# Norm weights moved from the mixers into the merge, x times D and two levels of scores moved to ScalarE, B transposed into another bank

## The chip, the cores and the metric

One core of a Trainium2 chip runs the whole program. The metric is device time in microseconds (us), median of several runs. The engines are called as in the profile: PE (TensorE, matrix products), DVE (VectorE), ACT (ScalarE), POOL (GpSimd), SP (the engine that here only issues transfers). "Bank" is one of PE's eight result banks in PSUM, 128 partitions by 512 float32.

## The reference

One layer of a hybrid decoder over 1024 tokens, width 1024: a token mixer with three branches (GLA, HGRN2, Mamba-2 SSD), merged by gates, and then a mixture of 32 experts. What this change touches, cut down:

```
# GLA and HGRN2, chunk by chunk (4 + 4 heads): o = intra-chunk scores @ v + decayed q @ state
y_gla  = rms_norm(o_gla,  gla_norm_w)  * silu(gr)
y_hgrn = rms_norm(o_hgrn, hgrn_norm_w) * silu(hg)
# SSD: 16 heads in 4 groups
y = ssd_chunked_scan(xs, dt, a_neg, bm, cm)
y = (y + ssm_d[:, None] * xs) * silu(sz)
y_ssm = rms_norm(y in 4 groups, ssm_norm_w)
g = sigmoid(gates)
merged = g0*(y_gla @ w_br_gla) + g1*(y_hgrn @ w_br_hgrn) + g2*(y_ssm @ w_br_ssm)
out = merged @ w_out
```

## The kernel before

The program runs in stages, each a block with its own streams of instructions per engine, ordered by hand; engines meet only by semaphores. The stages are: norm and decays, projection, `mixers`, `merge_and_route`, two expert stages, and `finish`. A float32 matrix product of the large stages is three products of rounded parts (hi*hi, hi*lo, lo*hi).

`mixers` walks over 8 chunks of 128 tokens (`body(c)` on each engine). Beside the mixers' own work PE computes the gate projection there: `fill(n)` issues the next n of its matmuls (128x512, line 1602). 24 of them make a half (`LATE_MM`), 8 a slot (`SLOT`), and a chunk has 15 slots between its own steps. All halves inside the chunks use bank 7, so the first matmul of a half waits until ACT has copied the half before out (`late(h)`, line 1258). After a copy ACT also rounds the next gate weights (`late_hi`, line 1251) or, for even h, issues the load of later ones (`late_load`, line 1246); that issue waits for DVE's `late_lo` (line 1375), and all that stands behind it in ACT's stream waits too. Odd chunks (1, 3, 5, 7) have the `late_load` at their first copy, even chunks the `late_hi`.

The steps of a chunk, in PE's order: the diagonal scores (1641); `intra(c-1, 1)`, second half of the SSD product of the chunk before (1669); levels 0 to 6 of the GLA/HGRN2 scores (`level`, 1627), a recursive halving in which level lv has blocks of h = 64 >> lv tokens; after level 2 the SSD product C*B (`cb`, 1690, into `ssm_ps`, bank 6); after level 3 the SSD state update (`ssm_state`, 1649); then `ssm_means(c-1)` (1657), a product with a matrix of equal entries that gives the mean squares for the last chunk's SSD norm; the transposes of B (1701) into the same bank 6; level 4; the transposes of x (1710) into `mid_ps` (banks 2 and 3); levels 5 and 6; transposes of k (1720); the outputs `o` (1730, 1731); `inter` (1735); the state update (1741); `intra(c, 0)`; the mean squares of the GLA/HGRN2 norm (1749).

For a level, DVE multiplies k and q by decays (`factors(lv)`, 1468 to 1470) and, when PE has its scores, copies those under the level's mask into `score` with a predicated copy (`scores_in(lv)`, 1486). DVE also does `gla_hgrn_out` (1439, 1443: times the reciprocal root, then eight instructions for weight and gate), `x_in_sum` (1405: eight instructions, x times D plus y), `z_gated` (1411), the subtraction `wd` (1517), the masked C*B (`cbm`, 1523) and `ssm_out` (1454: eight instructions, weight and reciprocal root). `wd` is the first to read `wmat` (in the profile `dn_raw_a`), which SP loads with a broadcast of `b_ssm` over 128 partitions (`load_bb`, 1 MB); SP issues it when PE has done `intra(c-1, 1)`. ACT computes the exponentials of each level (`relative`, 1270, 1271), the SSD squares (`ssm_squares`, 1283, wanted by `ssm_means`), the differences of `wmat` (1310), the copy of B's transposes (`bT`, 1330), the reciprocal roots (1275, 1277; 1287, 1289) and the squares of `o` (1337).

`merge_and_route` starts by splitting y into rounded parts: ACT `upper_y` (2118), DVE `rest_y` (2217), 16 pieces of 128x1024.

Of the kernel before, what the change touches and what calls it, by code (L numbers as in the profile page):

```python
# [957 lines left out]
def mixers(nc, io, dr, h_hi, h_lo, l_raw, l_hi, l_lo, w_place, xz_place, stored, early):  # L958
# [6 lines left out]
    NS = NL + 2  # L965
    CT = 6
    QT = 8
    NH = GLA_HEADS + HG_HEADS
    N_PAR = 5
# [4 lines left out]
    with ExitStack() as ctx:  # L974
# [35 lines left out]
        nw, nw_s, d_col = sb("nw", [P, NH]), sb("nw_s", [P, 8]), sb("d_col", [P, 8])  # L1010
# [39 lines left out]
        score_ready = sem("score_ready")  # L1050
        eb6_ready = sem("eb6_ready")
# [28 lines left out]
        intra_used = sem("intra_used")  # L1080
        xd_ready = sem("xd_ready")
# [21 lines left out]
        def _(sp):  # L1103
# [61 lines left out]
            sp.dma_start(nw[:, 0:4], io["gla_norm_w"].rearrange("(k p) -> p k", p=P)).then_inc(par_in, 16)  # L1165
            sp.dma_start(nw[:, 4:8], io["hgrn_norm_w"].rearrange("(k p) -> p k", p=P)).then_inc(par_in, 16)
            sp.dma_start(nw_s[:], io["ssm_norm_w"].rearrange("(k p) -> p k", p=P)).then_inc(par_in, 16)
            for a in range(2):
                sp.dma_start(d_col[a * HALF:(a + 1) * HALF, :], io["ssm_d"][a::2].unsqueeze(0).to_broadcast([HALF, 8]))\
                    .then_inc(par_in, 16)  # L1170
            for c in range(NCH):
# [68 lines left out]
        def _(act):  # L1240
# [50 lines left out]
            def body(c):  # L1291
# [4 lines left out]
                relative(c, 3)  # L1296
                relative(c, 4)
                late(h0)
# [16 lines left out]
                late(h0 + 1)  # L1315
                if c:
                    ssm_scale(c - 1)
# [9 lines left out]
                act.wait_ge(bT_ps_ready, c + 1)  # L1327
                if c:
                    act.wait_ge(hupd_ready, c)
                nc.scalar.copy(flat(bT[:]), ssm_ps).then_inc(bT_ready, 1)  # L1330
# [37 lines left out]
        def _(dve):  # L1368
# [68 lines left out]
            def gla_hgrn_out(c):  # L1437
# [13 lines left out]
            def ssm_out(c):  # L1451
                dve.wait_ge(rs2_ready, c + 1)
                for k in range(8):
                    ins = stt(yb[:, k, :], yt[:, k, :], nw_s[:, k:k + 1], rs2[:, k // 2, :], ALU.mult, ALU.mult)
                ins.then_inc(yb_ready, 1)

            def body(c):
                b, h0 = c % 2, PREFIX + PER_CHUNK * c

                def factors(lv):  # L1460
                    h, e = LEVELS[lv], ex[(NE * c + lv) % 3]
                    dve.wait_ge(e_ready, NE * c + lv + 1)
                    v = lambda x: x.rearrange("p (n w) -> p n w", w=2 * h)
# [8 lines left out]
                def diagonal_in(a):  # L1472
                    n = NS * c + a
                    dve.wait_ge(sc_ready, n + 1)
# [5 lines left out]
                def scores_in(lv):  # L1480
                    n, h = NS * c + 2 + lv, LEVELS[lv]
                    dve.wait_ge(sc_ready, n + 1)
                    dve.wait_ge(score_ready, n)
                    dve.sem_inc(passed, 1)
# [18 lines left out]
                scores_in(0)  # L1503
# [3 lines left out]
                scores_in(1)  # L1507
# [62 lines left out]
            for c in range(NCH):  # L1570
                if c == 1:
                    dve.wait_ge(par_in, 16 * N_PAR)
# [10 lines left out]
        def _(pe):  # L1583
# [31 lines left out]
            def level(c, lv):  # L1615
# [3 lines left out]
                pe.wait_ge(score_ready, NS * c + lv + 1)  # L1619
# [40 lines left out]
            def intra(c, s):  # L1660
                if s == 0:
                    pe.wait_ge(w_ready, c + 1)
                    pe.wait_ge(bT_ready, c + 1)
# [9 lines left out]
            def body(c):  # L1673
# [51 lines left out]
                pe.wait_ge(score_ready, NS * c + NS)  # L1725
# [60 lines left out]
def merge_and_route(nc, io, dr, ident, w_raw, y_raw, up_raw, up_at, xe, recs, recs_in, gather, early, kept_sem):  # L1786
# [32 lines left out]
    with ExitStack() as ctx:  # L1819
# [265 lines left out]
        def _(act):  # L2085
# [24 lines left out]
            def upper_y(p):  # L2110
# [7 lines left out]
                nc.scalar.copy(y_hi[:, q * PK:(q + 1) * PK, :], y_part(p)).then_inc(y_hi_ready, 1)  # L2118
# [36 lines left out]
            upper_w0(first, w0_loaded, w0_hi_ready)  # L2155
            for p in range(4):
                upper_y(p)
# [41 lines left out]
        def _(dve):  # L2199
# [13 lines left out]
            def rest_y(p):  # L2213
                dve.wait_ge(y_hi_ready, p + 1)
                q = p % PIECES
                ks = slice(q * PK, (q + 1) * PK)
                tt(y_lo[:, ks, :], y_part(p), y_hi[:, ks, :].bitcast(F32), ALU.subtract).then_inc(y_ready, 1)  # L2217
# [101 lines left out]
            rest_w0(first, w0_hi_ready, w0_ready)  # L2319
            for p in range(4):  # L2320
# [743 lines left out]
def build(nc, io, out):  # L3064
# [16 lines left out]
    with ExitStack() as ctx:  # L3081
# [11 lines left out]
        early = {name: kept_sem(f"early_{name}") for name in ("w0", "w0_rest", "y0", "y1")}  # L3093
# [75 lines left out]
```

## Time and profile before

| | us |
|---|---|
| median of 3 runs | 2035.61 |
| lowest and highest run | 2033.6, 2041.8 |
| span of the profiled execution | 2040.4 |
| mixer stage, chunks 0 to 7 (first diagonal to last `intra`) | 608.2 to 1066.2 |
| PE busy, whole span | 1925.7 (94%) |
| DVE busy | 1472.5 (72%) |
| ACT busy | 1048.0 (51%) |

The span runs from the first to the last recorded instruction. The profiled execution's own time is not listed apart from it; its span lies between the lowest and the highest run, 4.8 above the median. Busy time of an engine is the sum of its instructions; "idle before" in the rows below is the time in which an engine had nothing running just before an instruction, and the name behind the arrow is what ended that time. The granted clock is 1.00 when PE runs at 2.4 GHz and 0.50 at 1.2 GHz.

### The profile page before, as it was taken

The numbers are of one execution on the slowest core, as the hardware profiler recorded it, in microseconds if no ns is written. First come the engines' busy times: TensorE is split into PE (matmuls) and PEld (weight loads), VectorE is DVE, ScalarE is ACT, GpSimd is POOL, SyncE is SP. The second block draws the span as 40 slices with busy tenths as digits, with TensorE's granted clock in tenths as the row PEclk, the third lists the DMA queues.
The fourth block names the chain that finished last, engine by engine and source line by source line (L and its number), as shares of the span: only waits on it lengthen the run. The fifth ranks groups of instructions, "written<-read, shape, count | busy, mean of one in ns | idle before, by whom it ended". The sixth has DMA issues, their size and how long they took to land. (4 is left out here: it accounts for less than half of the span.)

```text
span 2040.4 us, 26797 instructions
## 1 busy us (share of the span) xinstructions
PE 1925.7 (94%) x10602; PEld 1576.7 (77%) x10603; DVE 1472.5 (72%) x1687; ACT 1048.0 (51%) x1234; POOL 218.3 (11%) x173
## 2 busy tenths in 40 slices
PE   6999999999999999999998999995999999999993
PEld 5789888888977777777776888874788888888881
DVE  5876467667227888788775656556889988999875
ACT  5234344444224545444444334223777887888763
POOL 3310000000030000000001000012122222222210
PEclk9999999999999999999998999997999999999996
DMA  5242332432355557656537654543999999999986
GB/s 168 86 145 73 114 104 97 131 104 93 107 145 158 151 160 168 167 127 152 160 115 282 206 204 182 229 178 138 349 376 384 389 386 385 389 386 387 387 331 259
DMA packets 212415, 436.11 MB, mean 214 GB/s; under 512 B 28018, under 2 KB 151042, under 8 KB 184770
## 3 DMA queue, kind: packets, MB, share of 16 engines
q1 hardware_dynamic: 179394, 355.68, 50.3%
q10 hardware_dynamic: 20864, 53.49, 7.5%
q0 software_dynamic: 12032, 25.22, 3.2%
q8 instruction: 85, 1.39, 0.3%
q14 instruction: 40, 0.33, 0.0%
HBM read 369.67 MB, written 81.43 MB: 221 GB/s over the span
## 5 line engine op out<-in xcount | busy, mean ns | idle before, releaser
L1602 PE MATMUL psum<-h_hi,l_hi 128*128 128x512 f32 x384 | 158.5, 413 | 4.9 <-PEq L58 3.3
L1602 PE MATMUL psum<-h_lo,l_hi 128*128 128x512 f32 x384 | 159.8, 416 | 0.0
L1602 PE MATMUL psum<-h_hi,l_lo 128*128 128x512 f32 x384 | 157.9, 411 | 0.0
L2741 DVE TENSOR_TENSOR gu_lo<-up_raw,gu_hi 128x2048 fp32r<-128x2048 f32 x64 | 146.3, 2288 | 13.2 <-ACT gu_hi L2684 13.2
L2684 ACT CAST gu_hi<-up_raw 128x2048 fp32r<-128x2048 f32 x64 | 122.1, 1909 | 35.0 <-PE u_ps L2813 35.0
L1258 ACT COPY l_out<-psum 128x512 f32<-128x512 f32 x48 | 28.1, 585 | 170.3 <-PE psum L1602 162.3
L2457 PE MATMUL mpsum<-y_hi,wb_hi 128*128 128x512 f32 x256 | 103.3, 403 | 10.1 <-DVE y_lo L2217 9.1
L2813 PE MATMUL g_ps<-gu_hi,xeT_hi 128*128 128x512 f32 x256 | 105.0, 410 | 5.8 <-DVE xeT_lo L2750 5.8
L806 DVE TENSOR_TENSOR w_lo<-w_raw,w_hi 128x512 fp32r<-128x512 f32 x90 | 61.9, 689 | 65.5 <-ACT w_hi L662 65.5
L662 ACT CAST w_hi<-w_raw 128x512 fp32r<-128x512 f32 x90 | 55.7, 622 | 91.9 <-PE ps L931 91.4
L2457 PE MATMUL mpsum<-y_lo,wb_hi 128*128 128x512 f32 x256 | 101.7, 397 | 0.0
L2457 PE MATMUL mpsum<-y_hi,wb_lo 128*128 128x512 f32 x256 | 101.6, 397 | 0.0
L2813 PE MATMUL g_ps<-gu_hi,xeT_lo 128*128 128x512 f32 x256 | 101.6, 397 | 0.0
L2813 PE MATMUL g_ps<-gu_lo,xeT_hi 128*128 128x512 f32 x256 | 101.4, 396 | 0.0
L2813 PE MATMUL u_ps<-gu_hi,xeT_lo 128*128 128x512 f32 x256 | 99.7, 389 | 0.0
L2813 PE MATMUL u_ps<-gu_hi,xeT_hi 128*128 128x512 f32 x256 | 99.6, 389 | 0.0
L2813 PE MATMUL u_ps<-gu_lo,xeT_hi 128*128 128x512 f32 x256 | 99.6, 389 | 0.0
L3123 POOL DMA_INDIRECT xe<-s_h,recs x32 | 88.6, 2770 | 32.4 <-PE xT_ps L2784 14.9
L1602 PEld LDWEIGHTS psum<-h_hi,l_hi 128*128 128x128 f32 x384 | 73.2, 191 | 21.9 <-issue 7.0
L2741 DVE TENSOR_TENSOR gu_lo<-gate_raw_a,gu_hi 128x2048 fp32r<-128x2048 f32 x32 | 73.4, 2293 | 22.2 <-ACT gu_hi L2684 22.2
L1602 PEld LDWEIGHTS psum<-h_hi,l_lo 128*128 128x128 f32 x384 | 73.5, 191 | 18.8 <-issue 3.3
L2662 POOL DMA_INDIRECT s_pairs<-ye,recs x32 | 41.4, 1293 | 431.3 <-ACT ye L2701 417.9
(465 smaller groups left out, 5419.0 us busy)
## 6 DMA issues: line engine op xcount, KB each, us to landing
up_raw<-moe SPq DMA_DIRECT2D x62, 1024.0 KB, 8.1
gate_raw_a<-moe SPq DMA_DIRECT2D x33, 1024.0 KB, 8.4
gate_raw<-moe SPq DMA_DIRECT2D x33, 1024.0 KB, 8.4
dn_raw_a<-moe SPq DMA_DIRECT2D x31, 1024.0 KB, 7.2
dn_raw<-moe SPq DMA_DIRECT2D x31, 1024.0 KB, 8.0
w_raw<-w_in SPq DMA_DIRECT2D x26, 1024.0 KB, 6.1
l_raw<-w_gates ACTq DMA_DIRECT2D x24, 512.0 KB, 5.4
s_gates<-l_out ACTq DMA_DIRECT2D x48, 256.0 KB, 4.0
```

The costliest lines, as they stand in the source:

```text
L662: nc.scalar.copy(slot_hi[g], source(n, g)).then_inc(hi_ready, 1)
L806: ins = tt(slot_lo[g], source(n, g), slot_hi[g].bitcast(F32), ALU.subtract).then_inc(split_ready, 1)
L1258: nc.scalar.copy(l_out[h % 2][:], psum[:, late_bank(h), :]).then_inc(l_evicted, 1)
L1602: ins = nc.tensor.matmul(psum[:, bank, :], w[t % 2][:, k, :], x[:, k, half * 512:half * 512 + 512], start=i == 0, stop=i == LATE_MM - 1, s ...
L2457: ins = nc.tensor.matmul(ps[:, br, :], w[:, k * P:(k + 1) * P], y[:, k, :], start=k == k0 and q == 0, stop=k == k1 - 1 and q == 2)
L2662: pool.indirect_dma_start(out=dr["pairs"], out_offset=bass.IndirectOffsetOnAxis(ap=recs[:, e, 1:2], axis=0), in_=ye[b][:], in_offset=None, ...
L2684: nc.scalar.copy(gu_hi[p][:], gu_raw[p][:]).then_inc(gu_hi_ready, 1)
L2741: nc.vector.tensor_tensor(gu_lo[p][:], gu_raw[p][:], gu_hi[p][:].bitcast(F32), ALU.subtract).then_inc(gu_ready, 1)
L2813: ins = nc.tensor.matmul(ps[:], x[:, (p - at) * GK + k, :], w[:, k, :], start=p == at and k == 0 and q == 0, stop=p == at + GU // 2 - 1 an ...
L3123: nc.gpsimd.indirect_dma_start(out=xe[e % 2][:], out_offset=None, in_=dr["h2"], in_offset=bass.IndirectOffsetOnAxis(ap=recs[:, e, 0:1], ax ...
```

## The change

- The three norm weights leave the mixers. `gla_hgrn_out` multiplies by the gate in one instruction instead of eight, and `ssm_out` likewise by the reciprocal root. The weights are loaded into `y_weight` and applied in the merge: `upper_y` becomes two scaled activations for a piece, `rest_y` two instructions of multiply and subtract.
- x times D: ACT scales `x_in` in place (`x_scaled`, eight activations, behind `late(h0+3)` and ahead of the squares of `o`), and DVE's `x_in_sum` becomes one addition.
- B's transposes go to the second half of `mid_ps` (bank 3) instead of bank 6. They wait for `ms_read` and no longer for `cbm_ready`. ACT's copy `bT` moves from behind the exponential of `wmat` to right behind `late(h0+1)`, ahead of `ssm_scale`. x's transposes now wait for `bT_ready`.
- `ssm_means` moves behind level 4.
- The scores of levels 0 and 1 are copied by ACT as plain blocks (`outer_scores`: one copy of 64 partitions x 512, two of 32 partitions x 256), behind `relative(3)` and `relative(4)`; DVE's `scores_in(0)` and `scores_in(1)` go. PE's levels 2 and 3 wait for ACT's copies (`outer_ready`) in place of DVE's, and DVE's `factors(2)` and `factors(3)` get a wait of their own for the level that last read their buffers.

```diff
-    N_PAR = 5
+    ON_ACT = 2
+    NM = NS - ON_ACT
+    N_PAR = 2
...
+            def outer_scores(c, lv):
+                h = LEVELS[lv]
+                act.wait_ge(sc_ready, NS * c + 2 + lv + 1)
+                act.wait_ge(score_ready, NM * c + 2)
+                if c:
+                    act.wait_ge(o_ready, c)
+                for n in range(CH // (2 * h)):
+                    j, i = slice(2 * h * n, 2 * h * n + h), slice(2 * h * n + h, 2 * h * (n + 1))
+                    ins = nc.scalar.copy(score[j, :].rearrange("p (a t) -> p a t", t=CH)[:, :, i],
+                                         sc_ps[lv % 2][j, :].rearrange("p (a t) -> p a t", t=HALF)[:, :, n * h:(n + 1) * h])
+                ins.then_inc(outer_ready, 1)
...
+            def x_scaled(c):
+                if c == 0:
+                    act.wait_ge(par_in, 16 * N_PAR)
+                act.wait_ge(xT_ready, c + 1)
+                for k in range(8):
+                    ins = nc.scalar.activation(x_in[:, k, :], x_in[:, k, :], ACT.Copy, scale=d_col[:, k:k + 1])
+                ins.then_inc(xs_ready, 1)
...
                 relative(c, 3)
+                outer_scores(c, 0)
                 relative(c, 4)
+                outer_scores(c, 1)
                 late(h0)
...
                 late(h0 + 1)
+                act.wait_ge(bT_ps_ready, c + 1)
+                if c:
+                    act.wait_ge(hupd_ready, c)
+                nc.scalar.copy(flat(bT[:]), mid_ps[:, 512:1024]).then_inc(bT_ready, 1)
                 if c:
                     ssm_scale(c - 1)
...
                 late(h0 + 3)
+                x_scaled(c)
...
             def x_in_sum(c):
                 dve.wait_ge(intra_used, 2 * c + 2)
-                for k in range(8):
-                    ins = stt(yt[:, k, :], x_in[:, k, :], d_col[:, k:k + 1], yt[:, k, :], ALU.mult, ALU.add)
-                ins.then_inc(xd_ready, 1)
+                dve.wait_ge(xs_ready, c + 1)
+                tt(yt[:], x_in, yt[:], ALU.add).then_inc(xd_ready, 1)
...
-                for h in range(NH):
-                    ins = stt(ya[:, h, :], g_in[:, h, :], nw[:, h:h + 1], ya[:, h, :], ALU.mult, ALU.mult)
-                ins.then_inc(ya_ready, 1)
+                tt(ya, g_in[:], ya, ALU.mult).then_inc(ya_ready, 1)
...
                     dve.wait_ge(e_ready, NE * c + lv + 1)
+                    if 2 <= lv < 2 + ON_ACT:
+                        dve.wait_ge(sc_ready, NS * c + lv + 1)
...
-                scores_in(0)
                 factors(2)
                 if c:
                     intra_in(c - 1, 1)
-                scores_in(1)
                 dec(i0 + 5)
...
                 if c:
-                    ssm_means(c - 1)
-                pe.wait_ge(cbm_ready, c + 1)
+                    pe.wait_ge(ms_read, c)
                 for g in range(SSM_GROUPS):
-                    ins = nc.tensor.transpose(ssm_ps[:, g * P:(g + 1) * P], bc_in[:, g, :], ident[:])
+                    ins = nc.tensor.transpose(mid_ps[:, 512 + g * P:512 + (g + 1) * P], bc_in[:, g, :], ident[:])
                 ins.then_inc(bT_ps_ready, 1)
                 fill(SLOT)
                 level(c, 4)
+                if c:
+                    ssm_means(c - 1)
                 fill(SLOT)
                 pe.wait_ge(x_loaded, 16 * (c + 1))
+                pe.wait_ge(bT_ready, c + 1)
...
-                nc.scalar.copy(y_hi[:, q * PK:(q + 1) * PK, :], y_part(p)).then_inc(y_hi_ready, 1)
+                for a in range(PK):
+                    k = q * PK + a
+                    ins = nc.scalar.activation(y_hi[:, k, :], y_part(p)[:, a, :], ACT.Copy, scale=y_weight[:, k:k + 1])
+                ins.then_inc(y_hi_ready, 1)
...
-                tt(y_lo[:, ks, :], y_part(p), y_hi[:, ks, :].bitcast(F32), ALU.subtract).then_inc(y_ready, 1)
+                for a in range(PK):
+                    k = q * PK + a
+                    ins = stt(y_lo[:, k, :], y_part(p)[:, a, :], y_weight[:, k:k + 1], y_hi[:, k, :].bitcast(F32), ALU.mult, ALU.subtract)
+                ins.then_inc(y_ready, 1)
```

How PE's stream stands around the moved steps in chunk 1, before: between the state update (1649) and level 4 (the next 1627) come two slots of filling (1602), and between the slots the means (1657, of the chunk before) and B's transposes (1701); the waits are those of the first instruction of a step.

```order
L1649 MATMUL psum<-xdt,bT 128x256 x3
L1602 MATMUL psum<-h_hi,l_lo 128x512
...
L1657 MATMUL psum<-y_out,mean_b 128x512 [waits ms_read,sq2_ready]
L1657 MATMUL psum<-y_out,mean_b 128x512
L1701 MATMUL psum<-ident_m,bc_in 128x128 [waits cbm_ready]
L1701 MATMUL psum<-ident_m,bc_in 128x128 x3
L1602 MATMUL psum<-h_lo,l_hi 128x512
```

And the same place in the changed kernel, where 1676 is the state update, 1624 the filling, 1726 B's transposes, 1654 a level and 1684 the means.

```order
L1676 MATMUL psum<-xdt,bT 128x256 x3
L1624 MATMUL psum<-h_hi,l_lo 128x512
...
L1726 MATMUL psum<-ident_m,bc_in 128x128 [waits ms_read]
L1726 MATMUL psum<-ident_m,bc_in 128x128 x3
L1624 MATMUL psum<-h_lo,l_hi 128x512
...
L1654 MATMUL psum<-q_lv,k_lv 64x2x32 [waits score_ready,qk_ready]
```

The means now stand behind level 4, and B's transposes wait for something that ACT did at the chunk's start.

ACT's stream of chunk 1 in the changed kernel, from the exponentials of level 3 to the squares of the SSD output:

```order
L1273 ACTIVATE ex<-ex 128x48x8 [waits d_ready]
L1274 ACTIVATE ex<-ex 128x48x8
L1284 COPY score<-psum 64x8x64 [waits o_ready,score_ready,sc_ready]
L1273 ACTIVATE ex<-ex 128x96x4 [waits d_ready]
L1274 ACTIVATE ex<-ex 128x96x4
L1284 COPY score<-psum 32x8x32 [waits o_ready,score_ready,sc_ready]
L1284 COPY score<-psum 32x8x32
L1261 COPY l_out<-psum 128x512 [waits l_stored0,l_done]
L1263 DMA s_gates<-l_out 128x512 [waits l_evicted]
L1249 DMA l_raw<-w_gates 128x1024 [waits l_split]
L1273 ACTIVATE ex<-ex 128x192x2 [waits d_ready]
L1306 ACTIVATE y_out<-yt 128x1024 [waits yt_ready]
```

The three copies (1284) are new there; the order of the rest is as before.

## Rows read from the trace of the kernel before

**Rows 1.** stretches, chunks 1 to 7: length, busy by engine, clock, DMA, GB/s

```profile
660.34:718.69 58.35, 55.94 (x447) 43.02 (x446) 48.15 (x82) 27.96 (x52) 0.00 (x0) 0.97 0.54 151
718.69:776.72 58.03, 55.52 (x448) 43.61 (x447) 47.21 (x81) 27.15 (x51) 0.00 (x0) 0.97 0.56 163
776.72:834.98 58.26, 55.85 (x448) 43.11 (x447) 48.14 (x82) 27.97 (x52) 0.00 (x0) 0.97 0.63 151
834.98:893.33 58.35, 55.55 (x447) 43.60 (x446) 47.24 (x81) 27.16 (x51) 0.00 (x0) 0.97 0.61 160
893.33:951.30 57.97, 54.47 (x449) 42.45 (x448) 48.22 (x82) 27.96 (x52) 0.00 (x0) 1.00 0.62 153
951.30:1009.50 58.20, 55.55 (x449) 43.56 (x448) 47.17 (x81) 27.17 (x51) 0.00 (x0) 0.97 0.65 162
1009.50:1066.00 56.50, 54.09 (x447) 42.51 (x446) 43.37 (x73) 26.33 (x48) 0.00 (x0) 1.00 0.34 105
```

**Rows 2.** waits of PE in the mixer stage: us, times, longest

```profile
PE psum L1657 <- ACT y_out L1283: 9.6, 4, 2.4
PE psum L1701 <- DVE cbm L1523: 9.1, 4, 2.8
```

**Rows 3.** timeline of PE, chunks 3 and 4: start, duration, idle before

```profile
797.61 3.58 PE L1657 MATMUL psum<-y_out,mean_b 128*128 128x512 f32 x4 [2.41 <-ACT y_out L1283]
...
849.59 1.99 PE L1649 MATMUL psum<-xdt,bT 128*128 128x256 f32 x8
853.28 1.88 PE L1657 MATMUL psum<-y_out,mean_b 128*128 128x512 f32 x4
857.96 0.66 PE L1701 MATMUL psum<-ident_m,bc_in 128*128 128x128 f32 x4 [2.80 <-DVE cbm L1523]
...
889.66 1.88 PE L1749 MATMUL psum<-y_out,mean_a 128*128 128x512 f32 x4
```

**Rows 4.** busy time by stretch, behind a wait of chunk 2

```profile
743.00:746.40 3.40, 3.40 (x29) 2.50 (x29) 3.40 (x7) 0.72 (x2) 0.00 (x0) 0.52 1.11 311
```

**Rows 5.** timeline of DVE, chunk 4

```profile
842.36 0.73 DVE L1486 COPY_PREDICATED score<-mask,psum 128x512 f32<-128x512 uint8 x1
...
848.45 2.20 DVE L1405 SCALAR_TENSOR_TENSOR yt<-gate_raw_a,d_col,yt 128x128 f32<-128x128 f32 x8
850.69 1.22 DVE L1411 TENSOR_TENSOR yt<-yt,gate_raw_a 128x1024 f32<-128x1024 f32 x1
853.33 0.18 DVE L1517 TENSOR_TENSOR wd<-dn_raw_a,b_dt 128x16 f32<-128x16 f32 x1 [1.41 <-DMA dn_raw_a<-s_b_ssm]
...
855.62 0.55 DVE L1470 TENSOR_TENSOR q_lv<-q_in,ex 128x384 f32<-128x384 f32 x1
```

**Rows 6.** timeline of ACT, chunk 3

```profile
786.84 0.58 ACT L1258 COPY l_out<-psum 128x512 f32<-128x512 f32 x1 [3.33 <-PE psum L1602]
...
795.61 0.56 ACT L1270 ACTIVATE ex<-ex 128x384 f32<-128x384 f32 x1 [8.19 <-DVE l_lo L1375]
...
796.51 1.04 ACT L1283 ACTIVATE y_out<-yt 128x1024 f32<-128x1024 f32 x1
...
798.76 2.45 ACT L1310 ACTIVATE dn_raw_a<-dn_raw_a,b_dt 128x128 f32<-128x128 f32 x8
...
823.07 1.02 ACT L1337 ACTIVATE y_out<-psum 128x1024 f32<-128x1024 f32 x1 [1.47 <-PE psum L1731]
```

**Rows 7.** issues of load_bb, chunks 3, 4, 5, then all: size, us to landing

```profile
dn_raw_a<-s_b_ssm SPq DMA_DIRECT2D x1, 1024.0 KB, 14.9
...
dn_raw_a<-s_b_ssm SPq DMA_DIRECT2D x1, 1024.0 KB, 16.3
...
dn_raw_a<-s_b_ssm SPq DMA_DIRECT2D x1, 1024.0 KB, 18.4
...
dn_raw_a<-s_b_ssm SPq DMA_DIRECT2D x8, 1024.0 KB, 16.0
```

**Rows 8.** timeline of PE, start of the merge

```profile
1095.08 0.76 PE L2457 MATMUL mpsum<-y_hi,wb_hi 128*128 128x512 f32 x1 [9.07 <-DVE y_lo L2217]
```

More of the change, by code:

```diff
@@ L955, in late_bank, with mixers @@
     return 7
-def mixers(nc, io, dr, h_hi, h_lo, l_raw, l_hi, l_lo, w_place, xz_place, stored, early):
+def mixers(nc, io, dr, h_hi, h_lo, l_raw, l_hi, l_lo, w_place, xz_place, y_weight, stored, early):
     LEVELS = [64 >> n for n in range(7)]
@@ L1050, in mixers @@
         score_ready = sem("score_ready")
+        outer_ready = sem("outer_ready")
         eb6_ready = sem("eb6_ready")
@@ L1080, in mixers @@
         intra_used = sem("intra_used")
+        xs_ready = sem("xs_ready")
         xd_ready = sem("xd_ready")
@@ L1170, in _ @@
                     .then_inc(par_in, 16)
+            for (k0, k1), name in (((0, 4), "gla_norm_w"), ((4, 8), "hgrn_norm_w"), ((8, 16), "ssm_norm_w")):
+                sp.dma_start(y_weight[:, k0:k1], io[name].rearrange("(k p) -> p k", p=P)).then_inc(early["yw"], 16)
             for c in range(NCH):
@@ L1452, in ssm_out @@
                 dve.wait_ge(rs2_ready, c + 1)
-                for k in range(8):
-                    ins = stt(yb[:, k, :], yt[:, k, :], nw_s[:, k:k + 1], rs2[:, k // 2, :], ALU.mult, ALU.mult)
-                ins.then_inc(yb_ready, 1)
+                grouped = lambda x: x.rearrange("p (g a) t -> p g a t", a=2)
+                tt(grouped(yb), grouped(yt[:]), rs2[:].unsqueeze(2).to_broadcast([P, SSM_GROUPS, 2, CH]), ALU.mult).then_inc(yb_ready, 1)
             def body(c):
@@ L1472, in diagonal_in @@
                 def diagonal_in(a):
-                    n = NS * c + a
-                    dve.wait_ge(sc_ready, n + 1)
+                    n = NM * c + a
+                    dve.wait_ge(sc_ready, NS * c + a + 1)
                     if n:
@@ L1480, in scores_in @@
                 def scores_in(lv):
-                    n, h = NS * c + 2 + lv, LEVELS[lv]
-                    dve.wait_ge(sc_ready, n + 1)
+                    n, h = NM * c + 2 + lv - ON_ACT, LEVELS[lv]
+                    dve.wait_ge(sc_ready, NS * c + 2 + lv + 1)
                     dve.wait_ge(score_ready, n)
+                    if lv == ON_ACT:
+                        dve.wait_ge(outer_ready, ON_ACT * (c + 1))
                     dve.sem_inc(passed, 1)
@@ L1618, in level @@
                 pe.wait_ge(qk_ready, NE * c + lv + 1)
-                pe.wait_ge(score_ready, NS * c + lv + 1)
+                if lv < ON_ACT:
+                    pe.wait_ge(score_ready, NM * c + lv + 1)
+                elif lv < 2 * ON_ACT:
+                    pe.wait_ge(outer_ready, ON_ACT * c + lv - ON_ACT + 1)
+                else:
+                    pe.wait_ge(score_ready, NM * c + lv - ON_ACT + 1)
                 ql = q_lv[lv % 2][:].rearrange("p (a n) -> p a n", n=HALF)
@@ L1724, in body @@
                 pe.wait_ge(q_dec_ready, c + 1)
-                pe.wait_ge(score_ready, NS * c + NS)
+                pe.wait_ge(score_ready, NM * c + NM)
+                pe.wait_ge(outer_ready, ON_ACT * c + ON_ACT)
                 if c:
@@ L2319, in _ @@
             rest_w0(first, w0_hi_ready, w0_ready)
+            dve.wait_ge(early["yw"], 48)
             for p in range(4):
@@ L3092, in build @@
         dn_first, gate_first = many(1, "dn_raw_a", [P, DK, D]), many(1, "gate_raw_a", [P, GK, FF])
-        early = {name: kept_sem(f"early_{name}") for name in ("w0", "w0_rest", "y0", "y1")}
+        early = {name: kept_sem(f"early_{name}") for name in ("w0", "w0_rest", "y0", "y1", "yw")}
+        y_weight = ctx.enter_context(nc.sbuf_tensor("y_weight", [P, 2 * KT], F32, side="right"))
         with ExitStack() as front:
@@ L3107, in build @@
             l_raw, l_hi, l_lo = ([l[:, b] for b in range(2)] for l in late_parts)
-            mixers(nc, io, dr, h_hi, h_lo, l_raw, l_hi, l_lo, flat(dn_first[0]), flat(gate_first[0]), stored, early)
+            mixers(nc, io, dr, h_hi, h_lo, l_raw, l_hi, l_lo, flat(dn_first[0]), flat(gate_first[0]), y_weight, stored, early)
         ident = ctx.enter_context(nc.sbuf_tensor("ident", [P, P], F32))
```

18 lines of the change are left out of this document (4 added, 14 removed).

## The prediction, made before the changed kernel ran

> **What bounds the kernel now.** I cut the trace into the mixer stage's chunks first. A chunk takes about 58 us and PE is busy in all but 2 to 4 us of it, while DVE and ACT have 10 and 30 us to spare [rows 1]. So PE's stream sets the time, and only its waits and slow stretches can be taken away. The list of waits gives 9.6 us in four waits of the means (1657) for ACT's squares and 9.1 us in four waits of B's transposes (1701) for DVE's masked C*B: 18.7 us in chunks 1 to 7 [rows 2]. The odd chunks wait at the means, the even ones at the transposes, chunk 5 at both (chunks 3 and 4: [rows 3]).
>
> The waits cost more than themselves. After chunk 3's wait the four records of the means take 3.58 us in place of 1.88 [rows 3]; after chunk 2's wait a stretch of 3.4 us ran at 0.52 of full speed, 1.2 GHz [rows 4]. A stretch at half clock gives back half its length, 1.7 us. The mean clock is 0.97 in five of the seven chunks and 1.00 in chunks 5 and 7 [rows 1], so I count five: 8.5 us. All told 18.7 + 8.5 = **27.2 us** can go here. Everything before and behind the stage is left alone, but for the start of the merge.
>
> What are the waited-for engines late with? In chunk 3 ACT stands 8.19 us before level 5's exponentials (1270) because the load it must issue first waits for DVE's l_lo; the squares (1283) come behind it, at 796.51, and PE starts the means at 797.61 [rows 3, 6]. In chunk 4 it is DVE that is late: eight instructions for x times D from 848.45, the product with z at 850.69, and then `wd`, which stands 1.41 us until the transfer of `load_bb` has landed, at 853.33 [rows 5]. Behind `wd` come the factors of level 4 (the last begins at 855.62) and the masked C*B that the transposes want.
>
> **The change part by part.**
>
> *Order on PE.* B's transposes no longer wait for DVE, but for a logarithm that ACT does at the chunk's start. The means move behind a slot, level 4, and need the squares some 3 us later relative to PE. With DVE's l_lo 3.3 us earlier (next paragraph) the squares of chunk 3 end near 794.3, and the means start near 798.4. Both old waits go: -18.7 us, and -8.5 with them.
>
> *DVE.* Each of the three eight-fold groups takes 2.20 us and becomes one instruction like the product with z, 1.22 [rows 5]: about 1.0 less each, 3 in a chunk. Two predicated copies of 0.73 (0.6 start to start) go: 1.2. Of these, 1.0 (`gla_hgrn_out`), 1.2 (scores) and 1.0 (`x_in_sum`) lie ahead of `wd`: DVE reaches it 3.3 us sooner. The rest comes late in the chunk, where DVE waits for PE anyway, and is worth nothing.
>
> *ACT.* The trace has no block copy of scores. The nearest row is the copy of a half, 128x512 in 0.58 us [rows 6]; the two small ones have half of that per partition, so I take 0.58 + 2 x 0.35 = 1.3, between 0.7 (if a start overlaps the one before) and, at most, two predicated copies of DVE for each level, 2.9. They sit where ACT stands idle 3.33 us before the half's copy [rows 6], so the cover is gone only above 3.3 us; then the half's copy, and the first filling of the next half that waits for it, come later by the excess. x times D: the eight activations of 1310 on the same shape take 2.45 us together [rows 6]; bounds 2.4 and 3.1. They stand ahead of the squares of `o`, for which ACT had 1.47 us of idle time in chunk 3, so these come 1.0 us (bounds 1.0 to 1.7) later than 823.07 + 1.02. PE reads them in the product at the chunk's end, which in chunk 4 starts at 889.66, 54.7 after the chunk's start; 824.1 is 47.4 after chunk 3's start [rows 1, 3, 6]. Seven us of cover: nothing. Copying B's transposes earlier is the same copy at another place, 0.58 us; it delays `ssm_scale`, for which PE's transposes of x wait. Counting ACT from `wd` (exponentials 1.3, differences 2.45, copy of the half 0.6, in odd chunks the cast 1.5, then 0.6 and the logarithm 0.7) gives 7.2 us after `wd`, against 7.4 on PE from the factors of level 4 (2.9 after `wd`; level 0.8, means 1.9, slot 1.9): 0 in my sum, up to 0.5 a chunk if a step is longer.
>
> *What is late next.* PE will reach level 4 earlier, and its factors stand behind `wd`, which waits for a transfer that DVE's gain cannot hasten. In chunk 4 PE would get there so: filling ended at 853.28, the transposes take 0.45 beyond, the next slot 1.9 (the slot between the state update's end at 851.4 and 853.28 [rows 3]): 855.65, which is 20.65 after the chunk's start at 834.98 [rows 1]. The factors end at 855.62 + 0.55 = 856.17, 2.84 after `wd`. Their load was issued 2.07 us after the chunk's start (853.33 less its 16.3 us to landing [rows 5, 7]). So level 4 waits 2.07 + d + 2.84 - 20.65 = d - 15.7 us, with d the time to landing: the median of the eight is 16.0, chunks 3 and 7 are at 14.9, and chunk 5 had 18.4 [rows 7]. That makes 0.3 in most chunks and 2.7 in chunk 5: about 4 us. In odd chunks one thing is added. ACT's load of gate weights, 512 KB, has gone out only behind DVE's l_lo, when `load_bb` of chunk 3 had landed (776.72 + 2.07 + 14.9 = 793.7, while the exponential behind the load's issue begins at 795.61 [rows 1, 6, 7]); 3.3 us earlier it falls into it. In the even chunks such a load goes out just ahead of `load_bb`, and d is 16.3 where chunk 3 has 14.9 [rows 7]: I take 1.3 for it in the odd chunks, that is 2 us more over the stage (chunk 3 and 7 have 0.8 of slack). Of 4 and 6 I take 5, and one stretch at half clock behind the longest wait, 1.7.
>
> On that point the Trainium skill has a rule ("DMA: Bandwidth & Descriptors", Queues, rings and completion order): each transfer engine goes round between the queues that have work, packet by packet, while one queue's descriptors are taken in order. By that rule x and z, issued 3.3 us earlier on SP's own queue, would not hold `load_bb` up, and ACT's load would. The trace agrees so far: the even chunks' d is longer by 1.4. If SP's loads shared too, the third rival below would be the sum.
>
> *Merge.* A piece's cast becomes two activations of half the length and DVE's subtraction two instructions; PE's 9.07 us of idle time there [rows 8] end with the first piece. I add 0.2 us, between 0 and 1: only the first piece is waited for, and half instructions cost a start more. The three small loads are the same number as before on the same queue, and the merge reads them 400 us later.
>
> **Sum.** -27.2 + 5 + 1.7 + 0.2 = -20.3 us. The profiled execution's span, 2040.4, would become 2020.1; the median of the runs lies 4.8 below that span, and from it I get 2035.6 - 20.3 = 2015.3, say **2015**.
>
> **The rivals.** 0.5% is 10.2 us, about what a measurement of this kernel can tell from no change.
>
> 1. *Forecast*: both waits go, a short one at level 4 comes. 2015, own range 2010 to 2022. Chance 0.58.
> 2. *Nothing is late next.* `load_bb` lands as in chunks 3 and 7, d = 14.9, since the stage's transfers spread otherwise. Then 27 us go: 2008.5. For it: two of seven chunks. Against it: five chunks are later. 0.14.
> 3. *`load_bb` is stretched part of the way* by x, z and the gate weights, all issued 3.3 us earlier: d grows by half of that in every chunk, 1.65, and the waits at level 4 sum to 4 + 7 x 1.65 - 1.6 = 14, with three stretches at half clock 19. The gain is 8: 2027.5, which is "same". For it: chunks 4 and 5 have the longer d, and in both x's load went out with DVE's product of z, before `load_bb` had landed [rows 5]. Against: chunk 4's d is explained by the load ahead of it. 0.15.
> 4. *Slower: `load_bb` is stretched by the whole 3.3 us.* Level 4 waits 4 + 7 x 3.3 - 1.6 = 25.5 us, each wait now as long as those of before, with seven stretches at half clock, 12: 37.5 come, 27.2 go, 2046. From d near 18 on it breaks even (16 us of waits and seven stretches), and from 19.5 on the kernel is slower by more than 0.5%. 0.06.
> 5. *ACT carries too much*: the score copies cost over 3.3 us, or `ssm_scale` comes 1 to 2 us late for x's transposes, and 1.5 us a chunk with some slow stretches eat 14: 2029, "same". ACT is only half busy [rows 1], but its waits are in order. 0.07.
>
> Faster by over 0.5% (below 2025.4): cases 1 and 2 and a part of 3 and 5, 0.78. Within: 0.16. Slower: 0.06. The range 2007 to 2028 leaves out case 4 and the ends of 2, 3 and 5.
>
> **What the profile will show.** Right: chunks of 54 to 55 us at a clock of 1.00 in most; no idle time before the means and before B's transposes; `wd` waiting 2 to 4 us for the transfer in every chunk; a wait of 0 to 1.5 us at level 4 for DVE's q_lv, in chunk 5 perhaps more; DVE's busy time 30 us less, ACT's 30 us more. Wrong: waits of over 2 us at level 4 (rivals 3, 4, with d of 18 and more), or at x's transposes for ACT's logarithm, or at the first filling behind a half for its copy (rival 5); or chunks that stay at 58 us.

## The result, and the profile after

The changed kernel takes 2025.68 us, the median of 4 runs (2025.02 to 2026.66); the kernel before took 2036.06 (2033.6 to 2041.8) in the same comparison. The ratio is 0.9944, 95% interval 0.993 to 0.9957: 10.4 us gained, about half of the 20.3 forecast. The profiled execution has a span of 2024.9 us.

First the page's busy times. PE carries what it carried before; DVE has lost work and ACT has taken it.

```profile
PE 1919.6 (95%) x10602; PEld 1577.3 (78%) x10603; DVE 1440.2 (71%) x1519; ACT 1080.9 (53%) x1338; POOL 216.5 (11%) x173
```

The stretches of chunks 1 to 7, to be laid beside [rows 1] (length, busy by engine, granted clock, DMA share, GB/s):

```profile
660.61:715.83 55.22, 53.75 (x448) 42.68 (x447) 43.79 (x59) 31.50 (x63) 0.00 (x0) 1.00 0.53 160
715.83:773.27 57.44, 55.37 (x448) 43.69 (x447) 42.88 (x58) 30.73 (x62) 0.00 (x0) 0.97 0.66 164
773.27:827.25 53.98, 53.76 (x447) 42.66 (x446) 43.80 (x59) 31.47 (x63) 0.00 (x0) 1.00 0.71 164
827.25:882.31 55.06, 53.78 (x448) 42.68 (x447) 42.65 (x58) 30.62 (x62) 0.00 (x0) 1.00 0.62 170
882.31:940.04 57.73, 55.42 (x448) 43.45 (x447) 43.98 (x59) 31.53 (x63) 0.00 (x0) 0.97 0.63 154
940.04:997.37 57.33, 55.43 (x447) 43.39 (x446) 42.87 (x58) 30.74 (x62) 0.00 (x0) 0.97 0.72 163
997.37:1052.00 54.63, 53.52 (x447) 42.67 (x446) 38.90 (x50) 29.82 (x59) 0.00 (x0) 1.00 0.41 109
```

They sum to 391.4 us where they summed to 405.7: 14.3 less. DVE is busy for 4.4 us less in a chunk, ACT for 3.5 more. The clock is 0.97 in three chunks (2, 5 and 6) where it was in five.

PE's waits in the mixer stage and up to the merge:

```profile
PE psum L1654 <- DVE q_lv L1494: 10.4, 7, 2.3
PE mpsum L2493 <- DVE y_lo L2251: 9.3, 1, 9.3
```

Both lines of [rows 2] are gone. In their place stands one, seven times: the products of level 4 (line 1654) wait for DVE's factors `q_lv`. The second line is the start of the merge, 0.2 more than in [rows 8]. Chunk 5 shows the new wait at its longest, first on PE, then on DVE (start, duration, idle before):

```profile
905.34 1.04 PE L1654 MATMUL psum<-q_lv,k_lv 128*64 128x64 f32 x24 [2.31 <-DVE q_lv L1494]
906.31 3.47 PE L1684 MATMUL psum<-y_out,mean_b 128*128 128x512 f32 x4
```

```profile
893.99 1.22 DVE L1431 TENSOR_TENSOR yt<-gate_raw_a,yt 128x1024 f32<-128x1024 f32 x1
895.25 1.22 DVE L1436 TENSOR_TENSOR yt<-yt,gate_raw_a 128x1024 f32<-128x1024 f32 x1
902.37 0.18 DVE L1541 TENSOR_TENSOR wd<-dn_raw_a,b_dt 128x16 f32<-128x16 f32 x1 [4.76 <-DMA dn_raw_a<-s_b_ssm]
902.59 0.72 DVE L1512 COPY_PREDICATED score<-mask,psum 128x512 f32<-128x512 uint8 x1
904.73 0.55 DVE L1494 TENSOR_TENSOR q_lv<-q_in,ex 128x384 f32<-128x384 f32 x1
```

DVE now has a single 1.22 us instruction where eight took 2.20 [rows 5]; it is ready at 897.6 and stands still at `wd` until `load_bb` has landed. Behind it PE waits 2.31 us, and the means that follow take 3.47 us: half clock, 1.2 GHz. The longest-waiting lines of DVE and ACT:

```profile
DVE wd L1541 <- DMA dn_raw_a<-s_b_ssm: 31.9, 7, 6.2
ACT wd L1329 <- DVE wd L1541: 20.7, 7, 5.3
```

Last, the load itself: first chunk 3's, then chunk 5's, then the seven of the stage with their median, to be laid beside [rows 7].

```profile
dn_raw_a<-s_b_ssm SPq DMA_DIRECT2D x1, 1024.0 KB, 15.9
...
dn_raw_a<-s_b_ssm SPq DMA_DIRECT2D x1, 1024.0 KB, 18.0
...
dn_raw_a<-s_b_ssm SPq DMA_DIRECT2D x7, 1024.0 KB, 17.1
```

Chunk by chunk, with before's for comparison (the loads from the same view of that chunk's first 6 us, `wd` from DVE's timeline, less the chunk's start):

| chunk | 1 | 2 | 3 | 4 | 5 | 6 | 7 |
|---|---|---|---|---|---|---|---|
| `load_bb` to landing, before | 15.8 | 16.0 | 14.9 | 16.3 | 18.4 | 16.1 | 14.8 |
| to landing, after | 17.1 | 17.7 | 15.9 | 16.9 | 18.0 | 17.5 | 16.8 |
| `wd` begins, after the chunk's start, before | 18.39 | 18.07 | 18.38 | 18.35 | 20.45 | 18.18 | 18.38 |
| `wd` begins, after | 19.20 | 19.81 | 17.94 | 19.03 | 20.06 | 19.63 | 18.85 |
| wait at level 4, after | 1.47 | 2.08 | 0.22 | 1.28 | 2.31 | 1.90 | 1.11 |
| the forecast's d - 15.7 | 1.4 | 2.0 | 0.2 | 1.2 | 2.3 | 1.8 | 1.1 |

The formula held to 0.1 us in all seven. Its input did not: d is 17.1 on average in place of 16.0. The rows of `wd` hold a surprise. DVE is ready for it 2.9 to 3.4 us sooner than before in every chunk, and still it begins 0.6 us later on average (19.2 in place of 18.6): in chunks 1, 3 and 7 of the kernel before it had not waited for the load at all.

### The profile page after: what moved, and what is told of

The parts are those of the page before. It is cut to its first block and busy times, and to the rows that moved or that the text cites. A ratio compares the mean times of both kernels' runs of the same rounds, so it can differ in the third digit from the quotient of the medians.

```text
span 2024.9 us, 26770 instructions
## 1 busy us (share of the span) xinstructions
PE 1919.6 (95%) x10602; PEld 1577.3 (78%) x10603; DVE 1440.2 (71%) x1519; ACT 1080.9 (53%) x1338; POOL 216.5 (11%) x173
## 5 line engine op out<-in xcount | busy, mean ns | idle before, releaser
L1624 PEld LDWEIGHTS psum<-h_lo,l_hi 128*128 128x128 f32 x384 | 73.2, 191 | 18.4 <-issue 4.1
```

The source lines that it names most:

```text
L1624: ins = nc.tensor.matmul(psum[:, bank, :], w[t % 2][:, k, :], x[:, k, half * 512:half * 512 + 512], start=i == 0, stop=i == LATE_MM - 1, s ...
```

## The experiments

Each stands beside runs of the kernel before on its own chip (medians 2038.0, 2038.4 and 2039.8), so the ratios are what to compare. "The stage" below is the mixer stage in each kernel's trace, from the first diagonal to the last `intra`: 459.0 us before, 442.8 in the changed kernel.

**Does `v`, loaded just ahead of `load_bb`, take its time?** The changed kernel with the two loads exchanged:

```diff
-                    sp.wait_ge(upd_ready, c + 1)
-                    load_v(n)
                     sp.wait_ge(intra_ready, 2 * c + 2)
                     load_bb(n)
+                    sp.wait_ge(upd_ready, c + 1)
+                    load_v(n)
```

> The changed kernel, with the load of v issued behind load_bb instead of ahead of it; nothing else is different, and v is wanted only some 35 us later. Theory (load_bb's landing sets level 4): v no longer stands ahead in the queue, so load_bb lands 1.5 to 2 us sooner after its issue (15 to 15.5 us in place of 17.1), the 10.4 us of waits at level 4 shrink to 1 to 3, the three stretches at half clock go with them: 2025.7 - 13 = about 2013. Rival (the rest of the chunk's time is lost elsewhere, in ACT's or DVE's order): no change within 2 us, level 4 waits for something else.

2028.56 us (2024.09 to 2030.1), ratio 0.9946 (0.9922 to 0.997). The loads take 16.1 to 17.7 us, the waits at level 4 sum to 10.9: as in the changed kernel, and not the 13 us less that were expected. The place of `v` does not matter. Whether `v` takes some of the load's time in either place is not shown: ahead of it, `v` still lands up to 3.8 us into the load, and behind it, 0.4 us later, it is in flight beside all of it.

**Do the loads issued behind it?** In the changed kernel SP holds x and z back until `load_bb` has landed, and with them all that stands behind them in its stream, first the store of y (`ya`), which otherwise goes out 1 us behind x:

```diff
                     sp.wait_ge(yt_ready, c + 1)
+                    sp.wait_ge(bb_loaded, 16 * (n + 1))
                     load_x(n)
                     load_z(n)
```

> The changed kernel, with SP waiting until load_bb has landed before it issues the loads of x and z and all that follows in its stream. Theory A (SP's own loads, issued 3.3 us sooner, stretched load_bb from 16.0 to 17.1): the time to landing goes back to 15 to 16 us, the waits at level 4 fall from 10.4 to about 4, one stretch at half clock stays: about 2016. Theory B (one queue is served in order, the gate weights of ACT's queue stretched it): load_bb unchanged at 17 us, 2025 to 2027. Rival to both: x comes too late for its transposes and PE waits there: above 2027.

2018.34 us (2014.55 to 2018.9), ratio 0.9897 (0.9869 to 0.9924). PE's and DVE's waits, and the load:

```profile
PE psum L1655 <- DVE q_lv L1495: 4.6, 6, 1.5
```

```profile
DVE wd L1542 <- DMA dn_raw_a<-s_b_ssm: 25.8, 7, 5.1
```

```profile
dn_raw_a<-s_b_ssm SPq DMA_DIRECT2D x7, 1024.0 KB, 16.2
```

The load lands 0.9 us earlier by the median, PE's wait falls from 10.4 to 4.6, no stretch at half clock is left in chunks 1 to 7, and 7 us come back by the medians, 9 in the stage (433.7 us). By chunk the loads take 16.2, 16.7, 15.9, 16.3, 17.1, 16.1 and 15.4 us: less than in the changed kernel in six of the seven, the same in chunk 3. The kernels of the next experiment agree: the median is 16.2 us where x and z go out as late as before (`order_only`), and 17.4 where they go out as early as in the changed kernel (`work_only`). So what SP issues later on its own queue did stretch the load ahead of it; which of x, z and the store does it is not shown. That disagrees with the use which the prediction made of the Trainium skill ("DMA: Bandwidth & Descriptors", Queues, rings and completion order): from descriptors taken in order on one queue it concluded that later ones would not hold an earlier one up.

**Which part of the change brings the gain?** `order_only` is the kernel before with the three moves on PE and ACT alone (B's transposes into the other bank without the wait for the masked C*B, their copy early, the means behind level 4); `work_only` is the changed kernel with those three undone. The core of the first:

```diff
                 if c:
-                    ssm_means(c - 1)
-                pe.wait_ge(cbm_ready, c + 1)
+                    pe.wait_ge(ms_read, c)
                 for g in range(SSM_GROUPS):
-                    ins = nc.tensor.transpose(ssm_ps[:, g * P:(g + 1) * P], bc_in[:, g, :], ident[:])
+                    ins = nc.tensor.transpose(mid_ps[:, 512 + g * P:512 + (g + 1) * P], bc_in[:, g, :], ident[:])
                 ins.then_inc(bT_ps_ready, 1)
                 fill(SLOT)
                 level(c, 4)
+                if c:
+                    ssm_means(c - 1)
```

> The kernel before, with only the order and the bank changed: B's transposes in bank 3, waiting for ms_read, ACT's copy of them moved forward, the means behind level 4. Norm weights, x times D and the scores stay as before. Theory (the reorder is the gain, and DVE's saved 3.3 us ahead of wd only lengthen its wait for load_bb): the old waits go here too, level 4 waits 0.3 to 1 us a chunk, load_bb stays near 16 us since x and z go out as late as before: 2016 to 2022, as fast as the whole change or faster. Rival (the shift of work off DVE is needed): DVE reaches wd too late, level 4 waits over 2 us a chunk with slow stretches: 2030 or more.

> The changed kernel with the old order and bank: B's transposes in bank 6 behind cbm_ready, the means ahead of them, ACT's copy at its old place. Norm weights, x times D and the two levels of scores stay moved. Theory (the shifted work alone buys little, since wd waits for load_bb): the odd chunks' wait at the means goes, but B's transposes wait 1.5 us in odd chunks and 3 to 4 in even ones for the masked C*B behind wd: 16 to 20 us of waits, 2030 to 2036. Rival (work off DVE is what pays): 2026 or less.

`order_only` takes 2025.11 us (2024.0 to 2026.29), ratio 0.9935 (0.9909 to 0.9961): as fast as the whole change, and its stage is as long, 443.1 us. It misses the expected 2016 to 2022, which did not have the waits for ACT in the list below. `work_only` takes 2041.39 (2038.35 to 2050.02), ratio 1.0022 (1.0007 to 1.0038): no gain, rather a small loss; its stage takes 460.0 us. PE's waits in the first, then in the second:

```profile
PE psum L1627 <- DVE q_lv L1470: 5.3, 6, 2.6
PE psum L1602 <- ACT l_out L1258: 4.4, 5, 1.1
...
PE psum L1711 <- ACT rs L1287: 1.5, 3, 0.5
```

```profile
PE psum L1728 <- DVE cbm L1547: 21.7, 7, 5.0
PE psum L1624 <- PEq L58: 3.3, 1, 3.3
PE psum L1624 <- ACT l_out L1261: 2.0, 2, 1.1
```

With the old order the faster DVE only reaches `wd` sooner and stands there, and PE, no longer held at the means, waits for the masked C*B in every chunk: 21.7 us in place of 18.7. All the gain came from the order. On top of it the shifted work came out even: it rid PE of the waits for ACT (4.4 and 1.5 us, of which 1.1 in chunk 0), and in exchange the stretched load made the waits at level 4 longer (10.4 us in place of 5.3) and left three stretches at half clock in place of one.

**Could a part of `load_bb` start sooner?** It is issued in two halves of the heads, the first behind the first product within the chunk that reads `wmat`, once in the changed kernel (`halves`) and once in `order_only` (`order_halves`):

```diff
-                    sp.wait_ge(intra_ready, 2 * c + 2)
-                    load_bb(n)
+                    for s in range(2):
+                        sp.wait_ge(intra_ready, 2 * c + 1 + s)
+                        load_bb(n, s)
```

> The changed kernel, with load_bb split by heads: the first 8 heads are loaded as soon as PE has done the first half of the SSD product (some 9 us sooner), the other 8 at the old time. Same bytes. Theory (load_bb is slow in itself, about 14 us for 1 MB whatever stands around it, and its landing is all that level 4 waits for): the second half lands 8 to 11 us after its issue, 11 to 13 us after the chunk's start; no wait at level 4, no stretch at half clock: 2025.7 - 15.5 = 2010, at most 2014. Rival (the transfer queue is full over the whole chunk, so an earlier issue only moves the packets of v and eb back): the second half still lands 16 us or more after the chunk's start, 2020 to 2026.

> The kernel before with the new order and bank alone (as order_only) and load_bb in halves; norm weights, x times D and scores stay as before. Theory: with the transfer out of the way DVE itself sets wd in every chunk, near 18.4 us after the start in odd and 17 in even chunks, so the shifted work is now worth something: waits of 0.4 at level 4, 1.1 at the first filling behind ACT's late copy and 0.5 at x's transposes in odd chunks, about 8 us in all: 2016 to 2021, that is 5 to 9 slower than the changed kernel with load_bb in halves. Rival (the shifted work is worth nothing even then): as fast as that kernel within 2 us.

2027.84 us (2023.62 to 2033.11), ratio 0.9938 (0.9917 to 0.9959), and 2025.89 (2023.56 to 2028.37), ratio 0.9933 (0.9913 to 0.9954). Neither gains on its parent, where 2010 and 2016 to 2021 were expected. The fourteen halves by their median, and PE's standing time in `halves` (level 4 is line 1657 there):

```profile
dn_raw_a<-s_b_ssm SPq DMA_DIRECT2D x14, 512.0 KB, 17.7
...
PE psum L1657 <- DVE q_lv L1497: 5.8, 2, 3.3
PE psum L1719 <- issue: 4.1, 1, 4.1
```

A half takes as long to land as the whole did. But that is not the time of 512 KB alone: the second half goes out 7.6 us behind the first, which is in flight beside it for another 9.7 to 12.4 us, and from the first issue to the last landing the 1 MB takes 21 to 27 us. Nor do the halves fail everywhere. In chunks 1 to 3 the second ones land after 14.6 to 15.9 us, PE never waits, and a chunk takes 53.7 to 54.0 us. In chunks 4 to 6 they take 18.3 to 19.6 us. PE waits 2.5 us in chunk 4 and 3.3 in chunk 6; in chunk 5 it stands for 4.1 us amid C*B (line 1719), where the profile shows nothing that it waits for. Why these chunks differ is not shown. Together with the hold (`halves_hold`, the edits of both):

> Both: load_bb in halves, and x and z held until it has landed. Theory: the halves land before x and z are wanted, so the hold never bites: the same as halves alone within 2 us, about 2010. Rival (transfers of x and z are still in the second half's way without the hold): 4 or more faster than halves alone.

2018.99 us (2015.97 to 2025.45), ratio 0.9902 (0.9868 to 0.9935), waits at level 4 of 6.7 us: what the hold alone gives. The hold was expected to bring nothing here, and brings 9 us.

**Is the move of the scores worth something once x and z are held?** `hold_xz` with the scores of the two outer levels back on DVE:

```diff
-    ON_ACT = 2
+    ON_ACT = 0
...
-                outer_scores(c, 0)
                 relative(c, 4)
-                outer_scores(c, 1)
...
+                scores_in(0)
                 factors(2)
                 if c:
                     intra_in(c - 1, 1)
+                scores_in(1)
```

> The changed kernel with x and z held until load_bb has landed (as hold_xz, 2018.3), and the scores of levels 0 and 1 copied by DVE again as before. Theory (DVE stands 2 to 5 us before wd for the transfer in that kernel, so 1.2 us of copies ahead of it cost nothing): 2018 within 2 us, the idle time before wd 1.2 us shorter in each chunk, the waits at level 4 as in hold_xz. Rival (the copies matter): 2024 or more.

2017.41 us (2016.61 to 2018.44), ratio 0.9892 (0.9867 to 0.9918), the same as `hold_xz`. DVE's wait at `wd`:

```profile
DVE wd L1540 <- DMA dn_raw_a<-s_b_ssm: 14.8, 7, 3.3
```

DVE waits 11 us less there, about the time of the work that it has again (two predicated copies in a chunk, 0.73 us each [rows 5]). Moving the copies to ACT bought only standing time.

**Is it the size or the pieces of the transfer?** Each of its 2048 runs (128 partitions, 16 heads) has 512 bytes, since `b_ssm` is stored with time running through all chunks; from head to head the source steps by 4 KB. Stored chunk by chunk, a partition's 16 heads are one run of 8 KB; the bytes stay the same. The store, the staged copy and `load_eb` are adapted with it:

```diff
-        ("dt", [16, T], F32), ("b_ssm", [16, T], F32),
+        ("dt", [16, T], F32), ("b_ssm", [NCH, 16, CH], F32),
...
-                sp.dma_start(wmat, dr["b_ssm"][:, c * CH:(c + 1) * CH].unsqueeze(0).to_broadcast([P, SSM_HEADS, CH]))\
+                sp.dma_start(flat(wmat), dr["b_ssm"][c].rearrange("h t -> (h t)").unsqueeze(0).to_broadcast([P, SSM_HEADS * CH]))\
                     .then_inc(bb_loaded, 16)
```

It is put into all three orders: `wide` is the changed kernel with it, `order_wide` is `order_only`, `before_wide` the kernel before.

> The changed kernel, with b_ssm stored chunk by chunk ([8, 16, 128] in place of [16, 1024]), so that load_bb reads and writes one run of 8 KB per partition in place of 16 pieces of 512 bytes; the same 1 MB. Theory (load_bb's landing, slow because it is 2048 small broadcast packets, is all that level 4 waits for): it lands 5 to 9 us after its issue, wd never waits, no wait at level 4 and no stretch at half clock, chunks of 53.8: 2025.7 - 15.5 = 2010. Rival (the queue is full of other transfers, or the broadcast reads of one address are slow in any size): 15 us or more to landing, 2020 to 2026.

> The kernel before with the new order and bank alone, and the same storage of b_ssm. Theory: DVE now sets wd, at 17 to 18.4 us after the chunk's start; odd chunks wait 0.4 at level 4, 1.1 at the first filling behind ACT's late copy, 0.5 at x's transposes, even chunks nothing: 8 us over four odd chunks: about 2016 to 2018, 5 to 8 slower than the changed kernel with that storage, which is what the shifted work is worth once the transfer is out of the way. Rival (the shifted work is worth nothing): within 2 us of it.

> The kernel before with that storage of b_ssm and nothing else. Theory (before, the transfer was late by 1 to 2 us at wd in four chunks, and B's transposes behind wd took that over): the even chunks' waits at B's transposes fall from 2.5-2.8 to 1.1-1.4 and chunk 5's from 1.1 to 0, the odd chunks' waits at the means stay 2.4: 5 to 8 us less with one or two stretches at half clock gone, 2028 to 2033. Rival (transfers did not matter before at all): 2036 within 2.

| parent | ratio as it was | ratio with 8 KB runs |
|---|---|---|
| kernel before | 1 | 0.9953 (0.9938 to 0.9968), 2030.69 us |
| order alone | 0.9935 (0.9909 to 0.9961) | 0.9925 (0.9908 to 0.9941), 2023.57 us |
| whole change | 0.9944 (0.993 to 0.9957) | **0.9858 (0.984 to 0.9876), 2012.34 us** |

The parts do not add up singly: the storage alone gives 9.1 us by the medians, the change alone 10.4, and both together 27.5. `wide` (2007.32 to 2012.72) is the fastest kernel here. Its loads in the stage, and its stretch over chunks 1 to 7:

```profile
dn_raw_a<-s_b_ssm SPq DMA_DIRECT2D x7, 1024.0 KB, 6.0
```

```profile
660.00:1050.00 390.00, 390.00 (x3191) 308.90 (x3190) 306.30 (x408) 221.82 (x441) 0.00 (x0) 1.00 0.54 163
```

1 MB lands in 4.7 to 7.3 us, PE is busy for all of the 390 us at a clock of 1.00, and each chunk takes 53.72 us. In `order_wide` PE still has waits:

```profile
PE psum L1604 <- ACT l_out L1260: 4.3, 4, 1.1
PE psum L1604 <- PEq L58: 3.3, 1, 3.3
PE psum L1713 <- ACT rs L1289: 1.9, 4, 0.5
PE psum L1629 <- DVE q_lv L1472: 1.7, 4, 0.4
```

They make its odd chunks 56.3 us long, and its median lies 6 us above the expected 2016 to 2018. So the shifted work is worth something after all, once the transfer is out of the way: 11 us by the medians and 10.8 in the stage (438.0 and 427.2 us). The two spans (2015.1 and 2011.0) differ by only 4.1, since the stage of `wide` begins 4.4 us later (see the last section) and 2.2 us more are lost behind the start of the merge. In `before_wide` the means wait as before and the transposes less:

```profile
PE psum L1659 <- ACT y_out L1285: 9.6, 4, 2.4
...
PE psum L1703 <- DVE cbm L1525: 3.4, 3, 1.1
```

The first of these never hung on the transfer, the second did for 5.7 of its 9.1 us.

## Why the prediction was right in its direction and off in its size

- **The two old waits, -18.7**: right. Neither is left.
- **Stretches at half clock, -8.5 and +1.7**: five became three, not one. Each of the three stands behind a wait at level 4 (2.08, 2.31 and 1.90 us); behind waits of 1.47 us and less there is none. That is +5.1 in place of +1.7. The length of a wait does not decide it alone: in `before_wide` two of the four waits of 2.4 us have such a stretch behind them and two have none, and one of 3.0 us in `work_only` has none.
- **"What is late next"**: the place (level 4), the cause (`wd` behind `load_bb`) and the formula d - 15.7 were right.
- **The term "of 4 and 6 I take 5"** is where the sum failed. It measured 10.4, because d was mis-sized. The forecast let only ACT's gate weights stretch the load, in odd chunks, by 1.3. It grew in six of the seven chunks, even ones too, by 1.1 on average. `hold_xz` shows the cause: x, z and the store behind them, which DVE's gain sends out sooner. That is the third rival's mechanism at 1.1 us where the rival took 1.65. Its cost of 19 (14 of waits, three stretches) stands against 15.5 measured (10.4 + 5.1); the forecast had 6.7. Its time of 2027.5 was nearer than 2015. Two of the prediction's own signs for it came, too: waits of over 2 us at level 4, in chunks 2 and 5 (2.08 and 2.31, with d of 17.7 and 18.0).
- **"The trace agrees so far: the even chunks' d is longer by 1.4"**: a reading of chunk 4 against chunk 3 alone. Over all seven chunks of before, d is 16.1 on average in the even ones and 16.0 in the odd ones. In `hold_xz`, where the gate weights go out inside the load in odd chunks as they do in the changed kernel, the averages are 16.4 and 16.2. Chunks 3 and 7, the shortest of before, are 1.0 and 0.6 longer there; a general 1.3 for the gate weights in odd chunks does not appear, and no run moves them alone.
- **DVE, 3.3 us sooner at `wd`**: right as a time and, as the prediction said, unable to hasten the transfer. What it didn't see is that `wd` would then begin later than before, and that on top of the new order the shifted work would come out even: `order_only` is as fast.
- **ACT**: the block copies and x times D, by their lines (instructions, duration min/median/max in ns, first and last start); what the rows say follows behind them:

```profile
L1284 ACT COPY score<-psum x24: 344/364/567, 618.6 to 1005.8; 32x256 f32<-32x256 f32 x16, 64x512 f32<-64x512 f32 x8
```

```profile
L1299 ACT ACTIVATE gate_raw_a<-gate_raw_a,d_col x64: 384/387/402, 647.5 to 1040.8; 128x128 f32<-128x128 f32 x64
```

- In a chunk that is one copy of 0.57 and two of 0.36, 1.3 us, as taken; the eight activations have the duration of line 1310's. PE has no wait for ACT in chunks 1 to 7. The fifth rival is excluded.
- **Merge, +0.2**: measured 0.2 (9.26 for 9.07).
- **What the sum did not hold.** The spans differ by 15.5 us, the medians by 10.4. The profiled execution of before lay 5.7 us above the median of these runs, that of after 1.0. Taking 27.2 us of waits and slow stretches, read in one execution, off a median that was lower may have counted some of that execution's own slowness as gain. Which of its stretches the other executions lacked can't be seen, since they have no trace. Within the spans, chunks 1 to 7 gave 14.3, chunk 0 gave 2.1, the last 240 us 1.7; 0.2 went at the merge, and 2.4 were lost ahead of the stage (below). Of the 14.3, the terms above explain 11.7 (27.2 less 15.5). The rest is busy time of PE outside waits and slow stretches, 0.4 to 0.8 us less in each odd chunk; no row shows where it went.

## What to carry to other kernels

Ask of every wait that you remove what its engine, or the engine it stood for, waits for next, and find that wait's own input: here `wd` and a transfer of 16 us. Making DVE faster in front of it did not pay as things stood. It paid once the transfer was short (10.8 us in the stage), and it seems to pay once what is issued behind the transfer is held back: `hold_xz` has a stage of 433.7 us against 443.1 of `order_only`, though the hold was not run on `order_only` itself. Work sent to another engine or made shorter also sends its loads and stores out sooner, into the load that is already late; a hold of one semaphore gave back 7 us of that.

Before moving work around a slow load, look at how its source is laid out. Storing a scratch tensor in the order in which it is read back gave 13 us more on top of the change (by the medians; ratios 0.9944 and 0.9858 with their intervals apart). By itself it gave 9.1, since the two old waits at the means and the transposes stood behind it (9.6 and 3.4 us left in `before_wide`), and the change on top of it gave 18.4. Two improvements that each uncover the other's wait have to be measured together.

## What the runs showed of the hardware

- **How the source of a broadcast is laid out sets its time.** 1 MB read for 128 partitions took 14.8 to 18.4 us in runs of 512 bytes, in the kernel before and the changed one (61 GB/s at 17.1), and 4.7 to 7.3 in runs of 8 KB, in `wide` (175 GB/s at 6.0). The length of the runs and the step of 4 KB between them changed together, and how much each counts was not separated. The short transfer also lands before x and z are issued, but by `hold_xz` that is worth only about 1 us. Two halves in runs of 512 bytes, in flight together with other loads, took as long each as the whole (17.7 us by the median). The Trainium skill ("DMA: Bandwidth & Descriptors", Why small descriptors are slow (HBM only)) gives a fixed overhead of about 3 cycles beside one per 32 bytes. An estimate from it, 19 cycles for the 16 of 512 bytes, would be 1.2 times the time; measured were 2.8 times (17.1 and 6.0 us), and the measurement decides. What makes up the rest stays open.
- **Transfers issued later on the same queue stretch a load in flight**, by about 1 us for x, z and the store of y (17.1 us with them, 16.2 with them held). Whether `v` was issued 8.6 us ahead of the load or 0.4 us behind it made no difference (17.1 and 17.3).
- **Time lost before any changed code runs.** The mixer stage's first products start at 608.2 us in the kernel before and at 610.6 in the changed one, with the same waits of PE ahead of them. A stretch at half clock lies near 90 us, in the first stage, in the changed kernel and not before. The same 10 us of both, first the changed kernel, then before:

```profile
86.00:96.00 10.00, 10.00 (x32) 6.63 (x31) 9.79 (x5) 0.58 (x1) 6.96 (x2) 0.83 0.14 55
```

```profile
86.00:96.00 10.00, 10.00 (x38) 6.69 (x37) 9.49 (x5) 0.48 (x2) 7.30 (x2) 1.00 0.16 63
```

- PE is busy in all of both, with a clock of 0.83 in one. The profiled executions of six of the kernels (those of the changed family but `work_only` and `halves_hold`) have it and start the stage at 610.6 to 613.4; the others start it at 607.6 to 608.5. It is 2 to 6 us that no edit here explains; with one trace for each kernel it can't be said whether a kernel has it always. It is about as much as the differences between nearby kernels: comparisons of whole times finer than that are left open.
